# Linear-attention levels and diagonal in blocks of their own, and reordered stage starts, heads and merge operands, in a four-layer transformer kernel on one core

## The chip, the core and the metric

The kernel runs on one core of one Trainium2 chip. It is one program that computes a stack of four transformer layers. The metric is the device time of one execution in microseconds, lower is better; the median of several executions is compared. The engines are TensorE (PE, with its weight loads as PEld), VectorE (DVE), ScalarE (ACT), GpSimd (POOL) and SyncE (SP), which issues the transfers.

## What is computed

512 tokens of width 1024, float32 everywhere. The first block is a gated linear attention layer and a convolutional feed-forward layer, then a sparse attention layer (compressed keys, selected blocks, a window) and another convolutional feed-forward layer. The second block is two hybrid layers (four heads of differential attention and eight heads of stick-breaking attention side by side), each followed by a feed-forward layer. Each layer normalizes its input by its root mean square and adds its result to the residual x. The reference, cut to the mixers that the change touches:

```python
def gla_mixer(h, ...):                      # 4 heads, key width 128, value width 256
    q, k, v, r, a_low = split(h @ w_in)
    log_a = log_sigmoid(a_low @ w_alpha_up + b_alpha) / 16
    # b = cumulative sum of log_a over tokens, per head and key dimension
    # att[t, s] = sum_d q[t,d] * k[s,d] * exp(b[t,d] - b[s,d])   for s <= t
    ...
def hybrid_layer(x, ...):
    h = rms_norm(x, g_attn)
    dq, dk, dv, sq, sk, sv, gates = split(h @ w_in)
    # differential: softmax(q1 k1) v - lam * softmax(q2 k2) v, causal; then rms_norm
    # stick-breaking: z = q k / 8; a = exp(log_sigmoid(z) + sum over later keys of log_sigmoid(-z))
    merged = g_diff * (o_diff @ w_o_diff) + g_sb * (o_sb @ w_o_sb)
    x = x + merged @ w_out
    h2 = rms_norm(x, g_ffn)
    gate, up = split(h2 @ w_ffn_in)
    return x + (silu(gate) * up) @ w_ffn_out
```

## The kernel before, in words

**Layout.** Features lie on the 128 partitions and the 512 tokens in the free dimension, so x is eight tiles of 128 x 512. The stages run one after another: linear attention (gla), feed-forward, sparse attention (its keys and values, kv, then its queries and output), feed-forward, hybrid layer 0 (hyb0) and its merge, feed-forward, hybrid layer 1 (hyb1) and its merge, feed-forward.

**Weights.** All weight matrices are stored as 446 units of 128 x 1024, taken in a fixed order through a ring of four slots. SyncE issues the transfer of a unit into w_raw once the slot is free (s_used); POOL splits it into a high part w_hi and a remainder w_lo (L461, L464) and raises s_w. The activations are split likewise: XH and XL. A `tile` on TensorE is one unit: eight contraction blocks k, each of three matmuls of 128 x 512 into one bank (`product`, L488 to L490: high by XH, high by XL, low by XH).

**Start of a stage.** VectorE makes XL[k] block by block (L1657) and adds up the squares, ss (L1669), behind which `stats` (L504) sums ss over the partitions on TensorE. Its result gives rstd, by which every product of the stage is scaled when it is copied out of its bank. In kv, hyb0 and hyb1 the first tile waits for each XL[k] (s_xl), and `stats` stands behind tile 1.

**Linear attention.** The sum over s <= t inside a chunk of 128 tokens is split into seven levels: level lv pairs the odd and even halves of blocks of 128 >> lv tokens. For each level VectorE makes exponents (L1783, L1784), ScalarE takes the exponential, VectorE multiplies by queries and keys (`decayed`, L1789, L1790) into g_z, TensorE forms the products (L603) of every chunk (4) and head (4) at full width in banks 5 to 7, and VectorE places them into g_att through a mask (`place`, L1812). One level goes after each of the tiles 10 to 16; the same token with itself (`diagonal`, L613) comes after tile 17. Then TensorE turns the decayed keys (`end_keys`) and forms the outputs from g_att. In between VectorE copies the value tiles out (L1770) and TensorE turns them (L509).

**Hybrid layers.** TensorE runs 12 tiles, then 16 units of differential scores (n = 0 to 15), between which the groups of the further tiles are laid by `fill(t, part)`, 6 groups (one k each) a unit from tile 12 on. Then come eight stick-breaking heads. Head h is `s_scores`, two fill tiles 24+2h and 25+2h, a wait for `sp` (h_sp_lo, made by VectorE, L2249), the cumulative sums (L1090); ScalarE then takes the exponential. In heads 0 and 7 the tile 25+2h was cut: six groups ahead of the sums, two behind.

```python
cut = KT if 0 < h < SB_HEADS - 1 else 6
fill(25 + 2 * h, range(cut))
if h == 0:
    d_sumsq(DIFF_HEADS - 1)
pe.wait_ge(hs["sp"], k0 + h + 1)
```

A fill tile is copied out by VectorE (L2168, h_gate or h_raw), after a wait for its bank. The differential outputs h_od get their high part h_odh from ScalarE and the remainder h_odl from VectorE (L2258), four subtractions after the last head; the merge begins with them, then takes h_osl of the stick-breaking outputs. The engines run in program order, and semaphores order them among each other.

## Time and profile before

| what | value |
| --- | --- |
| median of 3 runs | 2874.49 us (2873.88 to 2876.15) |
| the profiled execution | 2872.57 us, of which the span of the trace is 2870.8 |
| TensorE | 2826.8 us busy, 98% of the span; weight loads 2278.6 |
| VectorE | 1346.0 us, 47% |
| ScalarE | 809.7 us, 28% |
| POOL | 2038.8 us, 71% |
| mean granted TensorE clock | 0.997 of full speed |
| transfers | 84 GB/s on average |

Busy time is an engine's own work in the span; the modelled end of a matmul lies somewhat after the moment at which the next one can start, so a timeline is better read from start to start. A row of the timeline has the start, the duration, the engine and line, the operands (out<-in) and in square brackets the idle time ahead of it with what ended it. A matmul of plain float32 operands is two records in the trace, so its counts there are twice those of the program (32 for a level's 16); one of split operands (XH, w_hi) is one.

### The profile page before, as it was taken

What the parts mean: (1) busy time and instruction counts of PE and PEld (TensorE: products, weight loads), DVE (VectorE), ACT (ScalarE), POOL (GpSimd) and SP (SyncE); (2) the same over time, 40 slices, a digit from 0 to 9 for tenths busy, and PEclk for the clock granted to TensorE, in tenths of its full rate; (3) what the DMA queues carried; (4) which work ended last, traced back from release to release, by engine and by line L of the source; (5) the groups of instructions that cost most, each with busy time, mean ns of one, the idle gap of its engine ahead of it and who ended that gap; (6) DMA issues with size and microseconds to landing.
All of it is one profiled execution on the core that took longest, in us unless ns stands there. A gap on an engine that the chain in (4) does not pass through costs nothing.

```text
span 2870.8 us, 38439 instructions
## 1 busy us (share of the span) xinstructions
PE 2826.8 (98%) x13860; PEld 2278.6 (79%) x13860; DVE 1346.0 (47%) x1980; ACT 809.7 (28%) x1477; POOL 2038.8 (71%) x2346
## 2 busy tenths in 40 slices
PE   9999999999999999999999999999999999999998
PEld 7888888878756888887777778888877777888887
DVE  3854666035576466613764453232065444623201
ACT  2242222023476222201434432110043444211101
POOL 6748989779635688877845577777786455877774
PEclk9999999999999999999999999999999999999999
DMA  4112222223200233222221222232222122222222
GB/s 156 61 49 92 99 97 95 95 91 116 81 2 2 74 97 100 96 95 95 82 67 59 67 88 96 95 99 99 95 92 78 59 67 73 90 99 97 95 95 95
DMA packets 66360, 242.54 MB, mean 84 GB/s; under 512 B 7488, under 2 KB 7616, under 8 KB 66240
## 3 DMA queue, kind: packets, MB, share of 16 engines
q1 hardware_dynamic: 66240, 240.95, 25.2%
q8 instruction: 74, 1.21, 0.2%
q14 instruction: 46, 0.38, 0.0%
HBM read 238.82 MB, written 2.10 MB: 84 GB/s over the span
## 4 chain that ended last, share of the span: by engine, by line
PE 90%; DVE 6%; POOL 2%; issue 1%; ACT 1%; DMA 0%; SPq 0%; DVEq 0%; ACTq 0%
PE bank L488 26%; PE bank L490 26%; PE bank L489 26%; POOL w_lo L464 1%; PE bank L912 1%; PE bank L837 1%; PE bank L1090 1%; PE bank L854 1%; DVE ss L1669 1%; PE bank L603 1%; PE bank L1005 1%; DVE XL L1657 1%; PE bank L1048 1%; PE bank L1061 1%; PE bank L986 1%
## 5 line engine op out<-in xcount | busy, mean ns | idle before, releaser
L464 POOL TENSOR_TENSOR w_lo<-w_raw,w_hi 128x256 fp32r<-128x256 f32 x1784 | 1482.5, 862 | 35.8
L461 POOL CAST w_hi<-w_raw 128x1024 fp32r<-128x1024 f32 x446 | 488.6, 1096 | 686.3 <-DMA w_raw<-weights_dram 685.6
L488 PE MATMUL bank<-XH,w_hi 128*128 128x512 f32 x2416 | 958.1, 397 | 9.0 <-DVE XL L1657 4.3
L490 PE MATMUL bank<-XH,w_lo 128*128 128x512 f32 x2416 | 942.4, 390 | 0.0
L489 PE MATMUL bank<-XL,w_hi 128*128 128x512 f32 x2416 | 941.9, 390 | 0.0
L488 PEld LDWEIGHTS bank<-XH,w_hi 128*128 128x128 f32 x2416 | 454.4, 188 | 113.6 <-issue 10.1
L490 PEld LDWEIGHTS bank<-XH,w_lo 128*128 128x128 f32 x2416 | 454.1, 188 | 96.4
L489 PEld LDWEIGHTS bank<-XL,w_hi 128*128 128x128 f32 x2416 | 454.7, 188 | 93.8 <-issue 2.6
L1680 DVE TENSOR_TENSOR X<-X,bank 128x512 f32<-128x512 f32 x64 | 43.8, 684 | 512.6 <-PE bank L490 512.3
L490 PE MATMUL bank<-hid_h,w_lo 128*128 (+1 forms) x704 | 273.9, 389 | 0.0
L488 PE MATMUL bank<-hid_h,w_hi 128*128 (+1 forms) x704 | 273.9, 389 | 0.0
L489 PE MATMUL bank<-hid_l,w_hi 128*128 (+1 forms) x704 | 273.9, 389 | 0.0
L1713 DVE TENSOR_TENSOR f_c<-bank,rstd 128x512 f32<-128x512 f32 x88 | 60.9, 692 | 293.3 <-PE bank L490 284.3
L1224 ACT ACTIVATE hid_h<-f_h 128x512 f32 x88 | 55.7, 632 | 397.0 <-DVE f_h L1728 397.0
L488 PEld LDWEIGHTS bank<-hid_h,w_hi 128*128 128x128 f32 x704 | 132.1, 188 | 27.6
L489 PEld LDWEIGHTS bank<-hid_l,w_hi 128*128 128x128 f32 x704 | 132.1, 188 | 27.5
L490 PEld LDWEIGHTS bank<-hid_h,w_lo 128*128 128x128 f32 x704 | 132.1, 188 | 27.2
L474 POOL TENSOR_SCALAR n_P<-n_P,n_st,n_gate 128x128 f32<-128x128 f32 (+3 forms) x112 | 69.8, 624 | 83.8 <-DVE n_st L2066 82.8
L1216 ACT ACTIVATE f_c<-f_u,par_sb 128x512 f32<-128x512 f32 x88 | 71.9, 817 | 169.2 <-DVE f_u L1713 169.1
L1222 ACT ACTIVATE f_s<-f_c 128x512 f32<-128x512 f32 x88 | 55.7, 633 | 192.4 <-DVE f_c L1713 147.4
L1730 DVE TENSOR_TENSOR hid_l<-f_h,hid_h 128x512 f32 x88 | 71.3, 810 | 81.0 <-ACT hid_h L1224 81.0
L1722 DVE SCALAR_TENSOR_TENSOR f_c<-f_u,par_sb,f_c 128x512 f32<-128x512 f32 x88 | 102.8, 1168 | 12.7 <-DVE f_c L1719 0.3
(348 smaller groups left out, 3374.7 us busy)
## 6 DMA issues: line engine op xcount, KB each, us to landing
w_raw<-weights_dram SPq DMA_DIRECT2D x446, 512.0 KB, 3.4
x_tok<-x_dram SPq DMA_DIRECT2D x4, 512.0 KB, 5.7
out_dram<-y_tok SPq DMA_DIRECT2D x4, 512.0 KB, 4.0
const_sb<-consts_dram SPq DMA_DIRECT2D x1, 834.0 KB, 11.6
par_sb<-params_dram SPq DMA_DIRECT2D x1, 665.0 KB, 10.0
masks_in<-masks_dram SPq DMA_DIRECT2D x1, 640.0 KB, 12.6
y_gain<-gain_out_dram SPq DMA_DIRECT2D x1, 512.0 KB, 6.1
const_sb<-consts_dram SPq DMA_DIRECT2D x1, 129.0 KB, 2.1
```

The costliest lines, as they stand in the source:

```text
L461: nc.gpsimd.tensor_copy(w_hi[s][:, :, :], w_raw[s][:, :, :]).then_inc(s_hi, 1)
L464: ins = nc.gpsimd.tensor_tensor(w_lo[s][:, rows, :], w_raw[s][:, rows, :], w_hi[s][:, rows, :].bitcast(F32), ALU.subtract)
L474: nc.gpsimd.tensor_scalar(w, w, n_st[:, 1, m:m + 1], n_gate[:, i, col:col + 1], ALU.mult, ALU.mult)\
L488: nc.tensor.matmul(out_ap, w_hi[slot][:, j, :], xh, start=start, stop=False)
L489: nc.tensor.matmul(out_ap, w_hi[slot][:, j, :], xl, start=False, stop=False)
L490: return nc.tensor.matmul(out_ap, w_lo[slot][:, j, :], xh, start=False, stop=stop)
L1216: nc.scalar.activation(f_c[side][:, :], f_u[side][:, 2:T + 2], ACT.Identity, bias=par_sb[:, bass.ds(t + b0, 1)], scale=par_sb[:, bass.ds(t ...
L1222: nc.scalar.activation(f_s[:, :], f_c[0][:, :], ACT.Silu).then_inc(s_silu, 1)
L1224: nc.scalar.activation(hid_h[:, bass.ds(i * (2 * T) + p * T, T)], f_h[:, :], ACT.Copy)\
L1713: V.tensor_tensor(dst, bank[2 * p + side][:, :], rstd[:, :], ALU.mult).then_inc(s_u, 1)
L1722: V.scalar_tensor_tensor(f, f_u[side][:, 0:T], par_sb[:, bass.ds(c + w0, 1)], f, ALU.mult, ALU.add).then_inc(s_c2, 1)
L1730: V.tensor_tensor(hid_l[:, bass.ds(i * (2 * T) + p * T, T)], f_h[:, :], hid_h[:, bass.ds(i * (2 * T) + p * T, T)].bitcast(F32), ALU.subtract)\
```

## The change

**Levels and diagonal.** The products of a level no longer fill 128 x 128 squares of which a mask keeps a part. Level 0 is one block of 64 x 64 for each chunk and head, level 1 two blocks of 32 x 32, and levels 2 to 6 and the diagonal four blocks of 32 keys (32 x 16 and 32 x 32). The four blocks of a chunk and head go to the four groups of 32 partitions of the bank. A level then fits one bank. `place` copies levels 0 and 1 straight to g_att, and puts levels 2 to 6 and the diagonal through one masked copy each into the compact g_ac, from which `spread` writes four copies to g_att. ScalarE's and VectorE's waits count accordingly.

**Starts.** In kv, hyb0 and hyb1 the first two tiles are interleaved block by block, the second two blocks behind (`first_tiles`), and `stats` stands inside tile 2, ahead of its third block.

**Heads.** Two groups of tile 12 go ahead of the first differential scores; tile 25+2h is no longer cut; and VectorE makes the four h_odl in the last head ahead of the copy of tile 38.

The diff, cut to its core (waits of later steps left out; of `place` the removed lines stand in the functions above):

```diff
+GB = 32
...
+        g_ac = at("g_ac", [P, TT, H4, GB], F32, o_A + 25088)
...
+            def first_tiles(u, k_sem, k_base):
+                lag = 2
+                pe.wait_ge(s_w, u + 1)
+                for k in range(KT + lag):
+                    if k < KT:
+                        pe.wait_ge(k_sem, k_base + k + 1)
+                        mm = product(bank[0][:, :], u % RING, k, XH[:, k, :], XL[:, k, :], k == 0, k == KT - 1)
+                    if k == KT - 1:
+                        mm.then_inc(s_used, 1)
+                    if k == lag:
+                        pe.wait_ge(s_w, u + 2)
+                    if k >= lag:
+                        j = k - lag
+                        mm = product(bank[1][:, :], (u + 1) % RING, j, XH[:, j, :], XL[:, j, :], j == 0, j == KT - 1)
+                mm.then_inc(s_used, 1)
+            def tile(u, b, xh, xl, k_sem=None, k_base=0, norm=None):
                 pe.wait_ge(s_w, u + 1)
                 for k in range(KT):
+                    if k == 2 and norm is not None:
+                        stats(norm)
...
                 def level(lv):
                     pe.wait_ge(gs["Z"], lv + 1)
-                    for pair in range(2):
-                        m = 2 * lv + pair
-                        if m >= 3:
-                            pe.wait_ge(gs["ev"], 2 * m - 4)
-                        for c in (2 * pair, 2 * pair + 1):
-                            for h in range(H4):
-                                z = g_z[lv % 2][:, h, c * P:(c + 1) * P]
-                                odd = z.rearrange("p (n two e) -> p n two e", two=2, e=P >> (lv + 1))[:, :, 1, :]
-                                to = c % 2 * 2 * P + h * P // 2
-                                mm = nc.tensor.matmul(bank[5 + m % 3][:, to:to + P // 2], z, odd, start=True, stop=True)
+                    m = lv + 1 if lv else 0
+                    if m >= 3:
+                        pe.wait_ge(gs["ev"], m - 2)
+                    for c in range(TT):
+                        for h in range(H4):
+                            z, n = g_z[lv % 2][:, h, c * P:(c + 1) * P], c * H4 + h
+                            if lv == 0:
+                                to = n % 8 * 64
+                                mm = nc.tensor.matmul(bank[5 + c // 2][0:64, to:to + 64], z[:, 0:64], z[:, 64:P],
+                                                      start=True, stop=True)
+                            elif lv == 1:
+                                for b in (0, 64):
+                                    mm = nc.tensor.matmul(bank[7][b:b + GB, n * GB:(n + 1) * GB], z[:, b:b + GB],
+                                                          z[:, b + GB:b + 2 * GB], start=True, stop=True)
+                            else:
+                                for b in range(0, P, GB):
+                                    odd = z[:, b:b + GB].rearrange("p (n two e) -> p n two e", two=2, e=P >> (lv + 1))[:, :, 1, :]
+                                    mm = nc.tensor.matmul(bank[5 + m % 3][b:b + GB, n * GB // 2:(n + 1) * GB // 2],
+                                                          z[:, b:b + GB], odd, start=True, stop=True)
+                        if lv == 0 and c % 2:
+                            mm.then_inc(gs["mm"], 1)
+                    if lv:
                         mm.then_inc(gs["mm"], 1)
...
                 def diagonal():
+                    pe.wait_ge(gs["ev"], LEVELS - 1)
                     for c in range(TT):
-                        m = 2 * LEVELS + c
-                        pe.wait_ge(gs["ev"], 2 * m - 4 if c < 3 else 4 * LEVELS + 1)
                         for h in range(H4):
-                            cols = slice(c * P, (c + 1) * P)
-                            mm = nc.tensor.matmul(bank[5 + m % 3][:, h * P:(h + 1) * P], g_k[:, h, cols], g_q[:, h, cols],
-                                                  start=True, stop=True)
-                        mm.then_inc(gs["mm"], 1)
+                            n = c * H4 + h
+                            for b in range(0, P, GB):
+                                cols = slice(c * P + b, c * P + b + GB)
+                                mm = nc.tensor.matmul(bank[7][b:b + GB, n * GB:(n + 1) * GB], g_k[:, h, cols], g_q[:, h, cols],
+                                                      start=True, stop=True)
+                    mm.then_inc(gs["mm"], 1)
...
                 for t in range(U_NSA_KV):
                     if t >= 4:
                         pe.wait_ge(ns["evac"], t - 3)
-                    tile(KV_UNIT[t], t % 4, XH, XL, s_xl if t == 0 else None, 8 * PREP[2])
-                    if t == 1:
-                        stats(2)
+                    if t == 0:
+                        first_tiles(KV_UNIT[0], s_xl, 8 * PREP[2])
+                    elif t > 1:
+                        tile(KV_UNIT[t], t % 4, XH, XL, norm=2 if t == 2 else None)
...
                 for t in range(12):
...
-                    tile(u0 + t, t % 5, XH, XL, s_xl if t == 0 else None, 8 * PREP[n0 if ly else MID])
-                    if t == 1:
-                        stats(n0 if ly else MID)
+                    if t == 0:
+                        first_tiles(u0, s_xl, 8 * PREP[n0 if ly else MID])
+                    elif t > 1:
...
+                fill(12, (0, 1))
...
-                    for p_ in range(6 * n, 6 * n + 6):
+                    for p_ in range(6 * n if n else 2, 6 * n + 6):
...
-                    cut = KT if 0 < h < SB_HEADS - 1 else 6
-                    fill(25 + 2 * h, range(cut))
+                    fill(25 + 2 * h)
...
-                    if cut < KT:
-                        fill(25 + 2 * h, range(cut, KT))
                     if h == 0:
                         s_scores(1)
...
                 def place(lv):
+                    if lv == 0:
+                        for m in range(2):
+                            dve.wait_ge(gs["mm"], m + 1)
+                            V.tensor_copy(g_att[0:64, 2 * m:2 * m + 2, :, 64:P].rearrange("p c h t -> p (c h) t"),
+                                          bank[5 + m][0:64, :].rearrange("p (q t) -> p q t", t=64)).then_inc(gs["ev"], 1)
+                        return
+                    m = lv + 1
+                    dve.wait_ge(gs["mm"], m + 1)
+                    products = bank[5 + m % 3]
+                    if lv == 1:
+                        for b in (0, 64):
+                            ins = V.tensor_copy(g_att[b:b + GB, :, :, b + GB:b + 2 * GB].rearrange("p c h t -> p (c h) t"),
+                                                products[b:b + GB, :].rearrange("p (q t) -> p q t", t=GB))
+                        ins.then_inc(gs["ev"], 1)
+                        return
+                    if lv > 2:
+                        dve.wait_ge(gs["ev"], lv + 1)
+                    to = g_ac[:, :, :, :].rearrange("p c h t -> p (c h) t")
                     if lv < LEVELS:
+                        e = P >> (lv + 1)
+                        to = to.rearrange("p q (n two e) -> p q n two e", two=2, e=e)[:, :, :, 1, :]
+                        products = products[:, 0:8 * GB].rearrange("p (q n e) -> p q n e", q=16, e=e)
+                        mask = masks_bf[:, lv:lv + 1, 0:GB // 2].bitcast(U16).broadcast_to([P, 16, GB // 2])\
+                            .rearrange("p q (n e) -> p q n e", e=e)
+                    else:
+                        products = products[:, :].rearrange("p (q t) -> p q t", q=16)
+                        mask = masks_bf[:, lv:lv + 1, 0:GB].bitcast(U16).broadcast_to([P, 16, GB])
+                    V.copy_predicated(to, mask, products).then_inc(gs["ev"], 1)
+                def spread():
+                    dve.wait_ge(gs["ev"], LEVELS + 2)
+                    for b in range(0, P, GB):
+                        ins = V.tensor_copy(g_att[b:b + GB, :, :, b:b + GB].rearrange("p c h t -> p (c h) t"),
+                                            g_ac[b:b + GB, :, :, :].rearrange("p c h t -> p (c h) t"))
+                    ins.then_inc(gs["ev"], 1)
...
                 V.memset(g_att[:, :, :, :], 0.0)
+                V.memset(g_ac[:, :, :, :], 0.0)
...
+                spread()
                 evac(18)
...
+                    for k in range(4 if h == SB_HEADS - 1 else 0):
+                        dve.wait_ge(hs["odh"], 4 * ly + k + 1)
+                        V.tensor_tensor(h_odl[:, k, :], h_od[:, k, :], h_odh[:, k, :].bitcast(F32), ALU.subtract)\
+                            .then_inc(hs["odl"], 1)
                     evac(24 + 2 * h)
```

What each engine issues shows three places.

TensorE in the linear attention, around level 2; a row is an instruction with its operands, then output partitions by streamed columns, and how many such follow each other. Before:

```order
L489 MATMUL bank<-XL,w_hi_60 128x512
L490 MATMUL bank<-XH,w_lo_56 128x512
L509 MATMUL bank<-const_sb,g_vt 128x128 x4
L603 MATMUL bank<-g_z_87 128x64 x16
L488 MATMUL bank<-XH,w_hi_61 128x512
```

After:

```order
L493 MATMUL bank<-XL,w_hi_60 128x512
L494 MATMUL bank<-XH,w_lo_56 128x512
L532 MATMUL bank<-const_sb,g_vt 128x128 x4
L634 MATMUL bank<-g_z_87 32x16 x64
L492 MATMUL bank<-XH,w_hi_61 128x512
```

The 16 matmuls of 128 x 64 became 64 of 32 x 16; the tiles around them stand as before (level 0 is now 16 of 64 x 64, level 1 is 32 of 32 x 32, the diagonal 64 of 32 x 32).

VectorE in the same loop, from the placing of one level to the exponents two levels later. Before:

```order
L1812 COPY_PREDICATED g_att<-masks_bf,bank 128x8x32 x4
L1783 TENSOR_TENSOR g_z_88<-g_b 128x128x8
L1784 TENSOR_TENSOR g_z_88<-g_b 128x128x8
L1770 TENSOR_TENSOR g_vt<-bank,rstd 128x512
L1789 TENSOR_TENSOR g_z_88<-g_z_88,g_q 128x128x8
L1790 TENSOR_TENSOR g_z_88<-g_z_88,g_k 128x128x8
L1812 COPY_PREDICATED g_att<-masks_bf,bank 128x16x16 x4
L1783 TENSOR_TENSOR g_z_87<-g_b 128x256x4
```

After:

```order
L1842 COPY g_att<-bank 32x16x32 x2
L1820 TENSOR_TENSOR g_z_88<-g_b 128x128x8
L1821 TENSOR_TENSOR g_z_88<-g_b 128x128x8
L1807 TENSOR_TENSOR g_vt<-bank,rstd 128x512
L1826 TENSOR_TENSOR g_z_88<-g_z_88,g_q 128x128x8
L1827 TENSOR_TENSOR g_z_88<-g_z_88,g_k 128x128x8
L1858 COPY_PREDICATED g_ac<-masks_bf,bank 128x16x16
L1820 TENSOR_TENSOR g_z_87<-g_b 128x256x4
```

Four masked copies a level became one with the same number of elements in each row (levels 0 and 1: two plain copies); everything else kept its place.

TensorE at the start of kv. Before, the end of tile 1, the statistics matmul (bank 7) and tile 2:

```order
L488 MATMUL bank1<-XH_50,w_hi0_60 128x512
L489 MATMUL bank1<-XL_51,w_hi0_60 128x512
L490 MATMUL bank1<-XH_50,w_lo0_56 128x512
L504 MATMUL bank7<-ss_67,const_sb_64 128x512
L488 MATMUL bank2<-XH_50,w_hi1_61 128x512
L489 MATMUL bank2<-XL_51,w_hi1_61 128x512
L490 MATMUL bank2<-XH_50,w_lo1_57 128x512
```

After, a piece of the interleaved tiles:

```order
L492 MATMUL bank1<-XH_50,w_hi0_60 128x512
L493 MATMUL bank1<-XL_51,w_hi0_60 128x512
L494 MATMUL bank1<-XH_50,w_lo0_56 128x512
L492 MATMUL bank0<-XH_50,w_hi3_63 128x512
L493 MATMUL bank0<-XL_51,w_hi3_63 128x512
L494 MATMUL bank0<-XH_50,w_lo3_59 128x512
```

And after, the statistics inside tile 2:

```order
L492 MATMUL bank2<-XH_50,w_hi1_61 128x512
L493 MATMUL bank2<-XL_51,w_hi1_61 128x512
L494 MATMUL bank2<-XH_50,w_lo1_57 128x512
L527 MATMUL bank7<-ss_67,const_sb_64 128x512
L492 MATMUL bank2<-XH_50,w_hi1_61 128x512
```

Bank 0 and bank 1 now take turns, and the statistics come two groups of three matmuls later in the order. The same stands at the start of hyb0 and hyb1.

VectorE in the last stick-breaking head. Before:

```order
L2232 TENSOR_TENSOR h_sp<-h_sp,const_sb 128x256
L2168 TENSOR_TENSOR h_gate<-bank,rstd 128x512
L2241 COPY h_a<-h_sp 128x128
L2242 COPY h_a<-h_sp 128x128
L2243 TENSOR_TENSOR h_a<-h_sp 128x128
L2244 TENSOR_TENSOR h_a<-h_sp,h_a 128x256
L2246 CAST h_later_hi<-h_a 128x640
L2247 TENSOR_TENSOR h_later_lo<-h_a,h_later_hi 128x640
L2249 TENSOR_TENSOR h_sp_lo<-h_sp,h_sp_hi_184 128x1280
L2168 TENSOR_TENSOR h_gate<-bank,rstd 128x512
L2258 TENSOR_TENSOR h_odl<-h_od,h_odh 128x512 x4
L2262 TENSOR_TENSOR h_osl<-h_os,h_osh 128x512 x3
```

After:

```order
L2288 TENSOR_TENSOR h_sp<-h_sp,const_sb 128x256
L2293 TENSOR_TENSOR h_odl<-h_od,h_odh 128x512 x4
L2224 TENSOR_TENSOR h_gate<-bank,rstd 128x512
L2301 COPY h_a<-h_sp 128x128
L2302 COPY h_a<-h_sp 128x128
L2303 TENSOR_TENSOR h_a<-h_sp 128x128
L2304 TENSOR_TENSOR h_a<-h_sp,h_a 128x256
L2306 CAST h_later_hi<-h_a 128x640
L2307 TENSOR_TENSOR h_later_lo<-h_a,h_later_hi 128x640
L2309 TENSOR_TENSOR h_sp_lo<-h_sp,h_sp_hi_185 128x1280
L2224 TENSOR_TENSOR h_gate<-bank,rstd 128x512
L2318 TENSOR_TENSOR h_osl<-h_os,h_osh 128x512 x3
```

The four h_odl moved up, ahead of both gate copies and of h_sp_lo.

## Rows read from the trace of the kernel before

**Rows 1.** The page, busy time by engine: busy us, share of the span, instructions.

```profile
PE 2826.8 (98%) x13860; PEld 2278.6 (79%) x13860; DVE 1346.0 (47%) x1980; ACT 809.7 (28%) x1477; POOL 2038.8 (71%) x2346
```

**Rows 2.** Waits of TensorE: engine, line, releaser: us in total, times, longest.

```profile
PE bank L488 <- DVE XL L1657: 4.3, 9, 0.9
...
PE bank L488 <- DVE h_odl L2258: 2.9, 2, 1.5
```

**Rows 3.** Grouping by line and form, TensorE: busy us, mean ns | idle us.

```profile
L603 PE MATMUL bank<-g_z 128*128 128x64 f32 x224 | 25.8, 273 | 0.0
...
L613 PE MATMUL bank<-g_q,g_k 128*128 128x128 f32 x32 | 3.7, 275 | 0.0
```

**Rows 4.** Timeline of TensorE, levels 0 and 1: start, duration, [idle before].

```profile
83.85 3.68 PE L603 MATMUL bank<-g_z 128*128 128x64 f32 x32
87.34 0.47 PE L488 MATMUL bank<-XH,w_hi 128*128 128x512 f32 x1
...
93.35 3.68 PE L603 MATMUL bank<-g_z 128*128 128x64 f32 x32
```

**Rows 5.** Timeline of VectorE in the linear attention.

```profile
73.89 1.76 DVE L1828 MEMSET g_att<- 128x2048 f32 x1 [2.56 <-ACT g_b L1251]
...
88.37 2.06 DVE L1789 TENSOR_TENSOR g_z<-g_z,g_q 128x1024 f32<-128x1024 f32 x1 [1.38 <-ACT g_z L1255]
...
101.44 1.43 DVE L1812 COPY_PREDICATED g_att<-masks_bf,bank 128x256 f32<-128x256 uint16 x4
...
135.08 1.82 DVE L1789 TENSOR_TENSOR g_z<-g_z,g_q 128x1024 f32<-128x1024 f32 x1 [1.38 <-ACT g_z L1255]
136.82 1.75 DVE L1790 TENSOR_TENSOR g_z<-g_z,g_k 128x1024 f32<-128x1024 f32 x1
...
159.60 0.69 DVE L1770 TENSOR_TENSOR g_r<-bank,rstd 128x512 f32<-128x512 f32 x1 [2.57 <-PE bank L490]
```

**Rows 6.** Timeline of TensorE, compressed values of the sparse stage.

```profile
732.27 1.11 PE L783 MATMUL bank<-par_sb,n_hid 128*32 128x64 f32 x64
733.31 0.66 PE L509 MATMUL bank<-const_sb,n_raw 128*128 128x128 f32 x4
```

**Rows 7.** Timeline of TensorE, start of the kv stage.

```profile
622.71 0.39 PE L488 MATMUL bank<-XH,w_hi 128*128 128x512 f32 x1
...
637.53 1.12 PE L504 MATMUL bank<-ss,const_sb 128*128 128x512 f32 x2 [0.73 <-DVE ss L1669]
638.09 0.80 PE L488 MATMUL bank<-XH,w_hi 128*128 128x512 f32 x1
```

**Rows 8.** Timeline of TensorE, heads of the second hybrid layer.

```profile
2174.60 0.49 PE L1005 MATMUL bank<-h_dk,h_dq 64*128 64x128 f32 x4 [0.94 <-DVE h_raw L2168]
...
2288.68 0.84 PE L1090 MATMUL bank<-h_sp_hi,negtri_r 128*128 128x512 f32 x3 [1.20 <-DVE h_sp_lo L2249]
...
2293.39 0.66 PE L1048 MATMUL bank<-h_sqs,h_sk 64*128 64x512 f32 x1 [0.83 <-issue]
...
2402.03 0.85 PE L1090 MATMUL bank<-h_sp_hi,negtri_r 128*128 128x512 f32 x3 [0.42 <-DVE h_sp_lo L2249]
...
2407.39 0.47 PE L488 MATMUL bank<-h_odh,w_hi 128*128 128x512 f32 x1 [1.47 <-DVE h_odl L2258]
```

**Rows 9.** Timeline of VectorE, heads of the second hybrid layer.

```profile
2288.90 0.75 DVE L2200 SCALAR_TENSOR_TENSOR h_od<-bank,h_sub,h_ors 128x512 f32<-128x512 f32 x1 [0.27 <-ACT h_ors L1613]
2292.59 0.69 DVE L2168 TENSOR_TENSOR h_gate<-bank,rstd 128x512 f32<-128x512 f32 x1 [2.94 <-PE bank L490]
...
2397.57 0.69 DVE L2168 TENSOR_TENSOR h_gate<-bank,rstd 128x512 f32<-128x512 f32 x1 [4.71 <-PE bank L490]
...
2406.57 2.49 DVE L2258 TENSOR_TENSOR h_odl<-h_od,h_odh 128x512 fp32r<-128x512 f32 x4
```

**Rows 10.** TensorE after its longest wait for weights: timeline; then one stretch with its granted clock.

```profile
709.15 0.47 PE L488 MATMUL bank<-XH,w_hi 128*128 128x512 f32 x1 [1.71 <-POOL w_lo L464]
...
709.90:713.30 3.40, 3.40 (x10) 0.51 0.12 45
```

More of the change, by code:

```diff
@@ L117, in constants @@
     lv = np.zeros((P, 8, P))
-    for n in range(LEVELS):
+    key, token = np.arange(P)[:, None] % GB, np.arange(GB)[None, :]
+    for n in range(2, LEVELS):
         h = P >> (n + 1)
-        lv[:, n] = (a // (2 * h) == b // (2 * h)) & ((a // h) % 2 == 0) & ((b // h) % 2 == 1)
-    lv[:, 7] = a == b
+        level = (key // (2 * h) == token // (2 * h)) & ((key // h) % 2 == 0) & ((token // h) % 2 == 1)
+        lv[:, n, 0:GB // 2] = level[:, (np.arange(GB) // h) % 2 == 1]
+    lv[:, 7, 0:GB] = key == token
     masks = np.concatenate([lv, np.where(b <= a, 0.0, NEG)[:, None], np.where(a < b, 0.0, NEG)[:, None]], axis=1)
@@ L2253, in hybrid @@
                     evac(25 + 2 * h)
-                for k in range(4):
-                    dve.wait_ge(hs["odh"], 4 * ly + k + 1)
-                    V.tensor_tensor(h_odl[:, k, :], h_od[:, k, :], h_odh[:, k, :].bitcast(F32), ALU.subtract)\
-                        .then_inc(hs["odl"], 1)
                 for a in range(3):
```

29 lines of the change are left out of this document (6 added, 23 removed).

## The prediction, made before the changed kernel was timed

> **What bounds the kernel now.** I read the page first: TensorE has work in 2826.8 of the 2870.8 us [rows 1], so only two things can shorten the program: fewer microseconds of TensorE work, or fewer of its 44 us of idling. The list of what TensorE waits for comes second. Two of its rows are touched by the change as a whole, XL at the start of a stage (4.3 us) and h_odl at the merge (2.9 us) [rows 2]; the others it touches (ss, h_raw, h_sp_lo) stand in brackets in the timelines [rows 7, 8]. A wait costs more than its row says, because a matmul's modelled end lies about 0.16 us behind the moment at which the next could have started; I therefore count from start to start in the timeline. A group of three 512-column matmuls (one k of a tile) takes 0.68 us, a tile 5.45 us. Third, in the linear attention, the grouping by form and the timelines of TensorE and VectorE show whether the work taken away there is on the path.
>
> **Linear attention, TensorE.** A level is 32 records and takes 87.34 - 83.85 = 3.49 us, 109 ns a record, and the next begins at 93.35, a cycle of 9.50 us [rows 3, 4]. The seven levels are 224 records, the diagonal 32 at the same pace (its 3.7 us of busy time end in the drain; I take 3.5) [rows 3]. After the change level 0 is 32 records with 64 weight columns, level 1 is 64 with 32 columns on two strips, levels 2 to 6 and the diagonal are 128 each on four strips. The nearest row is L783: 64 records with 32 weight columns on four strips, all in 733.31 - 732.27 = 1.04 us, 16.3 ns each [rows 6]. I take that: 128 x 16.3 ns = 2.1 us for a level (1.4 saved) and for the diagonal (1.4 saved). Level 1 uses half as many strips: 64 x 32.5 ns = 2.1 us (1.4 saved). Level 0 has half the columns in both operands: half of 109 ns, 1.75 us (1.7 saved). On TensorE alone this is 1.7 + 6 x 1.4 + 1.4 = 11.5 us. Bounds: below, the products here stream 16 or 32 columns, not the 64 of L783, so down to a third of 2.1 us, 0.7; above, four strips share the 109 ns of a full record, 27.3 ns each, 3.5 us a level, which is no gain at all.
>
> **Linear attention, VectorE.** TensorE cannot have all of it, since each level waits for operands that VectorE makes. VectorE never waits for TensorE between 88 and 139 us; it starts its cycle at 88.37 and for the fifth time after that at 135.08, 9.34 us a cycle, barely shorter than TensorE's 9.50 [rows 5]. So the new cycle is VectorE's. Of it the change takes away only the placing: four predicated copies in 1.43 us, 0.33 from one start to the next [rows 5], become one of the same size. That is 1.0 us less for levels 2, 3 and 4, whose placing lies ahead of the last level. Levels 0 and 1 are placed by two copies of 512 columns out of a bank, about 0.62 us each like the row of h_gate (0.69 with its end) [rows 9]: 0.1 less each. The clearing of g_ac adds about 0.4, a quarter of g_att's 1.76 us for a quarter of its elements [rows 5]. Together the operands of level 6 are ready 3.0 + 0.2 - 0.4 = 2.8 us earlier: they were ready at 136.82 + 1.75 = 138.57 [rows 5], now at 135.8. Level 6 began at 83.85 + 6 x 9.50 = 140.85, so it begins 5.0 us earlier; it is itself 1.4 shorter and so is the diagonal. The diagonal's mask is now one copy, and the four copies of spread (at most 4 x 0.69 = 2.8 us) fall into a stretch in which VectorE idled 2.57 us and had three mask copies more [rows 5]; TensorE needs them only after a tile of 5.45 us, so I cost them at nothing. Without that cover they would cost up to 2.8. Term: 5.0 + 1.4 + 1.4 = **7.8 us**, bounds 3.4 (only levels 0 and 1 gain) and 10.6 (levels at 0.7).
>
> **Starts of the three stages (kv, hyb0, hyb1).** The first tile began at 622.71; two tiles without a wait are 16 x 0.68 = 10.9 us, 633.6; but the statistics matmul ran at 637.53, after XL in the first tile and then ss, and the work went on at 638.09 [rows 7]. Interleaving units 0 and 1 gives each XL[k] 1.36 us instead of 0.68 and hides those waits. (Unit 1 is needed from the third step on, 4 to 5 us earlier than before; should POOL not have split it yet, up to 2.3 us of that would vanish in the next wait.) But the sum of squares, the end of VectorE's chain, doesn't come earlier: the statistics stay at 637.53. What the change does gain is that the two tiles and two groups of tile 2 are done by then: 2 x 0.68 = 1.36 us. The XL wait turns into a longer ss wait, 637.53 - 635.0 = about 2.3 us against 0.9. Three stages: **4.1 us**; the rotation and weight chains behind follow TensorE's release of its tiles. Bounds 0 (they don't follow) and 3 x 2.5 = 7.5 (a shorter ss chain).
>
> **Heads.** The score products of the first differential head waited 0.94 us for h_raw, some 1.1 from start to start [rows 8]; two groups of fill(12) go ahead of it, 1.36 us of work, so the wait is filled and the scores begin 0.3 later: 1.1 saved per layer, **2.2 us**. In stick-breaking head 0 two groups move ahead of the wait for h_sp_lo, which ends at 2288.68 [rows 8] whatever TensorE does; they were 1.36 us behind it, and then s_scores(1) waited until 2293.39 for the gate tile, copied out at 2292.59 + 0.69 [rows 8, 9]. With the tile done before the sums, its copy follows d_out, which ran at 2288.90 [rows 9]; d_out's sum of squares is now issued 1.3 us later, so d_out runs at 2290.2 to 2290.9 and the copy to 2291.5. s_scores(1) starts at 2291.6 and I take a little less than the difference: 1.7 per layer, **3.4 us**, bounds 1.3 and 2.4.
>
> **End of the heads.** The last head's sums ran at 2402.03 after a wait of 0.42, then two groups, and the merge began at 2407.39 after 1.47 of waiting for h_odl [rows 8]. Now the groups fill the first wait, so the sums begin at 2402.8 and end 2.25 us later, and h_odl (2.49 us in four) is computed where VectorE idled 4.71 us for the gate tile [rows 9]. The merge can begin at 2405.05: 2.3 per layer, **4.7 us**. If the four subtractions ran later than that gap they would push h_sp_lo of head 7 by as much; the cover is 4.7 against 2.5.
>
> **The clock.** TensorE waited 1.71 us at 709.15, and for the next 3.4 us the granted clock was 0.51, the lower of its two levels, 1.2 GHz, which lost 1.7 us [rows 10]. The new ss waits of kv and hyb0 (2.3 us each) are longer than that one; the waits of 1.5 us and less in these rows were not followed by a fall. I count one such loss, **-1.7 us**. The Trainium skill, TensorE: Matmul & The Clock Gate, Part 1, says idling brings the lower clock and renewed activity releases it; the trace agrees, 0.51 after the wait.
>
> **The sum.** 7.8 + 4.1 + 2.2 + 3.4 + 4.7 - 1.7 = 20.5 us. The profiled execution took 2872.57 us in all (2870.8 span), 1.9 below the median of 2874.49. So 2872.57 - 20.5 = 2852.1, and as a median **2854.0 us**.
>
> **Rivals.**
> - *Small products are no cheaper than a quarter of a full one* (27.3 ns, above): the linear attention gives 3.4 instead of 7.8, 2858.4 us. For it: no row has so few streaming columns, and loading weights may set the pace. Against: L783's 16.3 ns. Chance 17%. The Trainium skill, TensorE: Matmul & The Clock Gate, section Back-to-back issue gap, has a floor of about 25 ns for 1 to 64 columns: by it a level takes 3.2 us, and the whole sum would be about 18 us. L783's 16.3 ns already lie under that floor, so the trace disagrees where strips are shared.
> - *The level loop is as fast as TensorE alone*, or no clock falls: 10.6 in the first term and no loss, 2849.5 us. Against: VectorE's 9.34 us cycle. 12%.
> - *More falls of the clock*: the loop gets seven waits of 1 to 2 us beside sparse small products; three or four more losses of 1.7 us, part of them hidden since TensorE waits there anyway: 2859 us. 10%.
> - *Slower*: the small products cost so much that the level loop outweighs the rest. The other parts save 12.7 after the clock; 6 blocks of 128 records lose that at (3.5 + 2.4) / 128 = 46 ns a record. One mechanism: each strip's weight load waits for the matmul before it instead of overlapping, so a record costs about 59 ns; a block is then 7.6 us, 4.1 over 3.5, and the program 2874.5 + 24.6 - 14.4 = 2885 us. Only L783 against it, but plainly. 2%.
> - *Nothing measurable* (several gains given back later, within 5.7 us): 3%.
> - The forecast itself, 2850 to 2858: 56%.
>
> **Numbers.** 0.2% of this kernel is 5.7 us, about what a measurement of it can tell from no change. Leaving 20% outside, I take 2849 to 2861. Faster 0.95, same 0.03, slower 0.02.
>
> **What would show it.** After: level records at some 16 ns and TensorE waiting for g_z in each level, 1 to 2 us; the diagonal's end 7.8 us earlier; the statistics matmul of kv still some 15 us behind the first tile, with one wait of about 2.3 us and none for XL; no wait for h_odl; s_scores(1) 2.9 us behind the first sum of head 0, not 4.7. I am wrong if the levels' records stand at 27 ns or more, if VectorE's cycle stays at 9.3 us, or if the clock is below 1.00 in the level loop.

## The result, and the profile after

| | median | runs | ratio to before, 95% interval |
| --- | --- | --- | --- |
| before | 2874.18 us | 4 (2869.63 to 2876.15) | |
| changed | 2856.53 us | 4 (2851.03 to 2858.23) | 0.9943 [0.993, 0.9955] |

The change made the kernel 17.7 us faster (13 to 20 by the interval); the forecast was 2854.0, in a range of 2849 to 2861. The profiled execution took 2858.23 us with a span of 2856.4, 14.4 less than that of before. The sum is right; the paths to it are only in part those of the forecast.

The page, busy time by engine, against [rows 1]:

```profile
PE 2811.7 (98%) x14468; PEld 2265.6 (79%) x14468; DVE 1338.3 (47%) x1963; ACT 809.8 (28%) x1477; POOL 2044.0 (72%) x2346
```

TensorE has 15 us less work, and about as much idling as before (44.7 us, before 44.0). What it waits for, against [rows 2] (engine, line, releaser: us, times, longest):

```profile
PE bank L1129 <- DVE h_sp_lo L2309: 4.1, 2, 2.1
PE bank L527 <- DVE ss L1706: 3.8, 2, 1.9
PE bank L492 <- POOL w_lo L468: 3.5, 5, 1.7
PE bank L634 <- DVE g_z L1827: 3.4, 3, 1.7
```

The waits for XL and h_odl are gone. In their place stand waits for ss (3.8, before 2.2), for h_sp_lo (from 3.3 in four to 4.1 in two) and for g_z, and more for the split weights (1.7 before).

**Linear attention.** Timeline of TensorE, levels 0, 2 and 3, the diagonal and the first outputs, against [rows 4]:

```profile
85.69 2.08 PE L625 MATMUL bank<-g_z 128*64 128x64 f32 x32 [0.19 <-DVE g_z L1827]
...
102.56 1.27 PE L634 MATMUL bank<-g_z 128*32 128x16 f32 x128 [1.16 <-DVE g_z L1827]
...
112.48 1.91 PE L634 MATMUL bank<-g_z 128*32 128x16 f32 x128 [1.75 <-DVE g_z L1827]
...
144.17 1.30 PE L649 MATMUL bank<-g_q,g_k 128*32 128x32 f32 x128
...
152.37 0.79 PE L684 MATMUL bank<-g_att,g_v 128*128 128x128 f32 x5
```

128 records of a level take 1.27 us, 9.9 ns each (level 3 ran at the lower clock); TensorE waits 1.16 and 1.75 us for g_z ahead of levels 2 and 3, 0.19, 0.20 and 0.53 ahead of levels 0, 1 and 6, and not at all ahead of 4 and 5. From the first level to the first outputs it was 76.86 us (83.85 to 160.71) and is now 66.68. Timeline of VectorE in this loop, against [rows 5]: an operation on g_z, the placing, another operation on g_z, this one beside POOL's work, and the spreading:

```profile
95.13 1.21 DVE L1820 TENSOR_TENSOR g_z<-g_b 128x1024 f32<-128x1024 f32 x1
...
112.35 0.43 DVE L1858 COPY_PREDICATED g_ac<-masks_bf,bank 128x256 f32<-128x256 uint16 x1
...
113.82 2.05 DVE L1821 TENSOR_TENSOR g_z<-g_b 128x1024 f32<-128x1024 f32 x1
...
148.34 3.88 DVE L1864 COPY g_att<-g_ac 32x512 f32<-32x512 f32 x4
```

The placing fell from 1.43 to 0.43 us as forecast, and VectorE's cycle from 9.34 to 8.53 us (`decayed` starts at 90.95 and for the fifth time after that at 133.60). An operation of `exponents` on 1024 columns is 1.21 or 2.05 us long. The spreading took 3.88, not the 2.8 that I allowed, and ended at 152.22, 0.15 us ahead of the outputs at 152.37; that it cost nothing was a near thing.

**Start of kv**, timeline of TensorE, against [rows 7]:

```profile
614.43 0.39 PE L492 MATMUL bank<-XH,w_hi 128*128 128x512 f32 x1
...
616.87 0.50 PE L492 MATMUL bank<-XH,w_hi 128*128 128x512 f32 x1 [0.24 <-POOL w_lo L468]
...
629.23 1.13 PE L527 MATMUL bank<-ss,const_sb 128*128 128x512 f32 x2 [1.85 <-DVE ss L1706]
...
700.28 0.77 PE L492 MATMUL bank<-XH,w_hi 128*128 128x512 f32 x1 [1.70 <-POOL w_lo L468]
```

From first tile to statistics it is 14.80 us (before 14.82), with waits of 0.24 and 1.85 in place of five, much as forecast. Two groups of tile 2 are done by then. The 0.24 is a wait for unit 1, which POOL had not split yet (0.73 in hyb0 and 0.30 in hyb1), as the forecast had allowed. But the last row shows that the wait for split weights later in the stage, 1.71 in [rows 10], is still there.

**End of the heads**, second hybrid layer. Timeline of VectorE, against [rows 9]:

```profile
2380.78 4.30 DVE L2293 TENSOR_TENSOR h_odl<-h_od,h_odh 128x512 fp32r<-128x512 f32 x4 [2.22 <-ACT h_odh L1612]
2385.01 0.68 DVE L2224 TENSOR_TENSOR h_gate<-bank,rstd 128x512 f32<-128x512 f32 x1
...
2387.18 1.54 DVE L2307 TENSOR_TENSOR h_later_lo<-h_a,h_later_hi 128x640 fp32r<-128x640 f32 x1
2388.64 2.01 DVE L2309 TENSOR_TENSOR h_sp_lo<-h_sp,h_sp_hi 128x1280 fp32r<-128x1280 f32 x1
```

Timeline of POOL beside it:

```profile
2380.35 4.19 POOL L468 TENSOR_TENSOR w_lo<-w_raw,w_hi 128x256 fp32r<-128x256 f32 x4
```

Timeline of TensorE, against [rows 8]:

```profile
2390.70 0.85 PE L1129 MATMUL bank<-h_sp_hi,negtri_r 128*128 128x512 f32 x3 [2.03 <-DVE h_sp_lo L2309]
...
2392.94 0.48 PE L492 MATMUL bank<-h_odh,w_hi 128*128 128x512 f32 x1
```

The four subtractions took 4.30 us and not 2.49; the gate copy behind them came 1.75 us late (2397.57 in [rows 9], less the 14.31 by which the kernel was ahead there, is 2383.26), h_later_lo took 1.54 and h_sp_lo 2.01 where they take 0.83 and 1.48 in the version with h_odl behind them (below). TensorE waited 2.03 for h_sp_lo, and the wait at the merge had only moved.

**By stretches.** The changed kernel was measured a second time, on another chip (2856.28 us, against 2872.73 for the kernel before; ratio 0.9946 [0.9933, 0.996]), and gave a second trace. I expected its stretches to repeat to 0.1 us outside the first 70 us, the falls of the clock and the starts, and a start to be 13 or 15 us in any kernel; the rival was that each kernel has a fixed value. The rival is refuted (hyb0's start took 13.36 us once and 15.04 the other time), but starts of 14.26 and 14.33 show that there are more than two values, and "heads" of layer a differed by 0.4.

The next table takes starts from the timelines of nine of the profiled executions, so that a late beginning in one of them doesn't count (us; "levels" is first level to g_osq, "start" first tile to statistics, "heads" from the matmul of h_lam to s_scores(1), "end" from there to the first merge matmul, a and b the two hybrid layers). Executions of like code differ mostly in "start" and where the clock fell.

| kernel | levels | start kv / a / b | heads a / b | end a / b |
| --- | --- | --- | --- | --- |
| before | 110.96 | 14.82 / 14.88 / 12.93 | 147.94 / 148.25 | 114.02 / 114.00 |
| changed | 100.87 | 14.80 / 13.36 / 14.93 | 145.79 / 145.22 | 113.92 / 113.85 |
| changed, second trace | 100.89 | 14.26 / 15.04 / 14.83 | 145.40 / 145.21 | 115.16 / 113.86 |
| levels alone | 101.33 | 12.87 / 12.93 / 14.95 | 148.32 / 147.56 | 114.01 / 114.02 |
| order alone | 110.94 | 14.00 / 14.24 / 14.92 | 145.24 / 145.33 | 114.96 / 113.77 |
| starts undone | 100.92 | 14.83 / 14.93 / 14.87 | 145.40 / 145.63 | 113.86 / 113.83 |
| h_odl last | 100.92 | 14.88 / 14.96 / 14.94 | 145.74 / 145.62 | 111.61 / 111.56 |
| h_odl behind h_sp_lo | 100.90 | 14.91 / 14.33 / 13.99 | 145.71 / 145.70 | 111.60 / 111.57 |
| copies for splits | 100.90 | 12.24 / 12.24 / 12.24 | 145.36 / 145.42 | 113.89 / 114.81 |

### The profile page after: what moved, and what is told of

Same layout as the page of the kernel before. It is cut to its first block, busy times and chain, and to the rows that moved or that the text cites. A ratio compares the mean times of both kernels' runs of the same rounds, so it can differ in the third digit from the quotient of the medians.

```text
span 2856.4 us, 39615 instructions
## 1 busy us (share of the span) xinstructions
PE 2811.7 (98%) x14468; PEld 2265.6 (79%) x14468; DVE 1338.3 (47%) x1963; ACT 809.8 (28%) x1477; POOL 2044.0 (72%) x2346
## 3 DMA queue, kind: packets, MB, share of 16 engines
q8 instruction: 79, 1.29, 0.2%
## 4 chain that ended last, share of the span: by engine, by line
PE 88%; DVE 6%; POOL 2%; ACT 2%; issue 1%; DMA 0%; SPq 0%; DVEq 0%; ACTq 0%
PE bank L492 26%; PE bank L494 25%; PE bank L493 25%; POOL w_lo L468 2%; PE bank L950 1%; PE bank L875 1%; PE bank L1129 1%; PE bank L892 1%; PE bank L1045 1%; PE bank L1088 1%; PE bank L1101 1%; DVE XL L1694 1%; PE bank L1026 1%; DVE ss L1706 1%; POOL w_hi L465 1%
## 5 line engine op out<-in xcount | busy, mean ns | idle before, releaser
L1759 DVE SCALAR_TENSOR_TENSOR f_c<-f_u,par_sb,f_c 128x512 f32<-128x512 f32 x88 | 105.6, 1200 | 12.8 <-DVE f_c L1756 0.3
## 6 DMA issues: line engine op xcount, KB each, us to landing
masks_in<-masks_dram SPq DMA_DIRECT2D x1, 640.0 KB, 12.8
```

The lines of the kernel that those rows point to most:

```text
L1759: V.scalar_tensor_tensor(f, f_u[side][:, 0:T], par_sb[:, bass.ds(c + w0, 1)], f, ALU.mult, ALU.add).then_inc(s_c2, 1)
```

## The experiments

**The two halves apart.** The first keeps of the diff only the hunks of the linear attention (masks, g_ac, `level`, `diagonal`, `place`, `spread` and their waits), the second only the others.

> The kernel before with the linear-attention part of the change alone. Theory: the parts add up, and this one is worth what the trace of the changed kernel shows between the first level and the last output, 10.1 us; about 2864. Rival, the forecast's term with VectorE's cycle as the bound throughout: 7.8 us, about 2866.4. If levels and reordering help each other only together, less than 7.

> The kernel before with the reordered starts, heads and merge operands alone. Theory: the trace of the changed kernel gives -0.9 in the kv stage, 4.7 in hybrid layer 0 and 2.5 in hybrid layer 1, together 6.4 us; about 2867.8. Rival, the forecast's terms 4.1 + 2.2 + 3.4 + 4.7 - 1.7 = 12.7 us: 2861.5.

Levels alone: 2860.89 us, ratio 0.9966 [0.9954, 0.9978], which is 9.8 us (6 to 13) and holds the theory's 10.1 as well as the rival's 7.8; only the traces part the two. Order alone: 2867.25, ratio 0.9986 [0.9977, 0.9995], which is 4.0 us (1.4 to 6.6); that leaves out the forecast's 12.7 us and just holds my 6.4 (0.9978). The table gives the levels 9.6 to 10.1 us in every kernel that has them, so they don't need the other half.

**The starts undone.** `first_tiles` and the statistics inside tile 2 taken back (the edit in kv; hyb0 and hyb1 likewise):

```diff
-                    if t == 0:
-                        first_tiles(KV_UNIT[0], s_xl, 8 * PREP[2])
-                    elif t > 1:
-                        tile(KV_UNIT[t], t % 4, XH, XL, norm=2 if t == 2 else None)
+                    tile(KV_UNIT[t], t % 4, XH, XL, s_xl if t == 0 else None, 8 * PREP[2])
+                    if t == 1:
+                        stats(2)
```

> The changed kernel with the first two tiles of kv, hyb0 and hyb1 one after the other again and the statistics behind tile 1. Theory: the interleaving is worth little, since it only reaches the statistics sooner (1.36 us a stage) and kv gives that back in waits for split weights; slower by 0 to 2 us, 2857.5. Rival, the forecast's term: slower by 4.1 us, 2860.6.

2857.74 us, ratio 0.9952 [0.9938, 0.9966]; 1.2 us over the changed kernel, or 2.6 by the two ratios (0.9943 there), less than these runs can tell. The traces are finer: from the statistics to the next common point (mid_ss in layer a, h_lam in b) the interleaving is worth 1.36 us (11.87 against 10.51, 28.20 against 26.83, but for the second trace of the changed kernel, where the clock fell ahead of mid_ss). In kv, from the statistics to the compressed values, five kernels with it take 94.2 to 95.3 us and three without 93.1 to 94.7: its 1.36 us is given back, as far as single executions show. In the changed kernel a wait of 0.57 us for w_lo at 664.84 has come ahead of the one of 1.70 that remained.

**h_odl moved.** Once back behind the last head, once directly behind h_sp_lo and ahead of the copy of tile 39 (the same lines, removed from where the change put them):

```diff
+                    for k in range(4 if h == SB_HEADS - 1 else 0):
+                        dve.wait_ge(hs["odh"], 4 * ly + k + 1)
+                        V.tensor_tensor(h_odl[:, k, :], ..., ALU.subtract).then_inc(hs["odl"], 1)
                     evac(25 + 2 * h)
```

> The changed kernel with the four subtractions for h_odl back behind the last head. Theory: they stand ahead of h_sp_lo of head 7, take 1.07 us each while POOL splits weights, and TensorE's last sums wait 2 us for h_sp_lo; put behind, the sums run at once (2.2 us earlier in each layer), and the subtractions are done beside the sums. 2856.5 - 4.4 = about 2852. Rival: the merge waits for h_odl again (1.5 us a layer as before), 2855 or more, no gain that can be told.

> The changed kernel with the four h_odl directly behind h_sp_lo of head 7, ahead of the copy of tile 39. Theory: the sums run 2.2 to 2.4 us earlier in each layer, and the 0.8 us that the merge lost in the run with the subtractions behind the copy is gone; 4.8 us less than the changed kernel, about 2851.7. Rival: beside the split of a weight unit a subtraction takes 1.07 to 1.2 us against 0.68 us of TensorE's work on it, so the merge still waits 0.8 a layer: 2853.3.

Last: 2854.09 us, ratio 0.994 [0.9926, 0.9953], which by time can't be told from the changed kernel (0.9943). Behind h_sp_lo: 2850.35, ratio 0.9926 [0.9912, 0.9939], against 2856.28 for the changed kernel on the same chip, 0.9946 [0.9933, 0.996]; the intervals still overlap, and the traces carry the reading. In both the end of the heads is 2.3 us shorter per layer. With h_odl last, the merge then ran 0.8 us slower (46.98 us to its first matmul of h_mh against 46.18), at the pace of subtractions of up to 1.23 us beside POOL (median 1.22, shortest 0.68); behind h_sp_lo that went too (46.20). Timeline of VectorE in the second one:

```profile
2379.03 1.48 DVE L2305 TENSOR_TENSOR h_sp_lo<-h_sp,h_sp_hi 128x1280 fp32r<-128x1280 f32 x1
2380.43 4.96 DVE L2311 TENSOR_TENSOR h_odl<-h_od,h_odh 128x512 fp32r<-128x512 f32 x4
```

Timeline of TensorE:

```profile
2381.35 0.74 PE L1129 MATMUL bank<-h_sp_hi,negtri_r 128*128 128x512 f32 x3
...
2383.49 0.48 PE L492 MATMUL bank<-h_odh,w_hi 128*128 128x512 f32 x1
```

No wait is left at the sums, nor at the merge, though the subtractions take even longer (4.96).

**Whose work stretches VectorE's.** For four units at each of the three starts POOL copies instead of subtracting, so that the products with w_lo of these units are of other numbers (`few` is true for them):

```diff
+                    if few:
+                        ins = nc.gpsimd.tensor_copy(w_lo[s][:, rows, :], w_raw[s][:, rows, :])
```

> The changed kernel in which POOL, for four units at the start of each of kv, hyb0 and hyb1, copies the unit in place of subtracting (this changes the products with w_lo of these units). Theory: VectorE's XL and ss are slowed by POOL's two-operand subtractions; with copies a start takes 13 us or less in all three stages, XL is 0.74 us each and TensorE's wait for ss is below 0.3. Rival: the chain's length has to do with VectorE or ScalarE alone; starts stay between 13 and 15 us, with the ss wait of 1.9 in some.

All three starts take 12.24 us (one execution, 2846.38 us). That is TensorE's own work, 18 groups of 0.68 us without a wait: VectorE's chain is no longer what a start waits for. Timeline of VectorE at the start of hyb1, in the changed kernel:

```profile
2093.18 0.67 DVE L1717 TENSOR_TENSOR X<-X,bank 128x512 f32<-128x512 f32 x1
2093.78 1.32 DVE L1694 SCALAR_TENSOR_TENSOR XL<-X,par_sb,XH 128x512 fp32r<-128x512 f32 x1
```

And in this one, first while POOL stands idle, then beside its copies:

```profile
2081.89 0.68 DVE L1721 TENSOR_TENSOR X<-X,bank 128x512 f32<-128x512 f32 x1
2082.48 0.74 DVE L1698 SCALAR_TENSOR_TENSOR XL<-X,par_sb,XH 128x512 fp32r<-128x512 f32 x1
...
2085.00 1.78 DVE L1698 SCALAR_TENSOR_TENSOR XL<-X,par_sb,XH 128x512 fp32r<-128x512 f32 x2
```

Timeline of POOL beside it:

```profile
2084.39 1.04 POOL L465 CAST w_hi<-w_raw 128x1024 fp32r<-128x1024 f32 x1 [2.17 <-DMA w_raw<-weights_dram]
2085.50 3.15 POOL L470 CAST w_lo<-w_raw 128x256 fp32r<-128x256 f32 x4
```

XL, which reads two operands from the SBUF, takes 1.32 us where it meets POOL's subtractions, 0.89 beside its copies and 0.74 beside nothing; X, whose second operand comes from a bank, is 0.67 beside the subtractions and 0.68 beside nothing. So my "0.74 each" held only where POOL stood idle, but POOL's subtractions stretch VectorE more than its copies do. No wait for ss is left.

**The statistics later.** On top of h_odl behind h_sp_lo, `k == 2` in `tile` became `k == 6`:

> The same with the statistics of kv, hyb0 and hyb1 ahead of the seventh instead of the third block of tile 2. Theory: four groups of TensorE (2.7 us) fill the wait of 1.9 us for ss; the kv stage gives it back in waits for split weights, so 1.9 to 3.8 us less than without, 2848 to 2850. Rival: rstd comes later, the first tiles are copied out later and the wait returns at tile 5; no gain, 2851.7.

2846.32 us, ratio 0.9913 [0.99, 0.9927], the fastest version: 10 us below the changed kernel and 4 below the one without this edit, whose interval overlaps. TensorE of its kv stage:

```profile
627.64 1.02 PE L527 MATMUL bank<-ss,const_sb 128*128 128x512 f32 x2
...
643.93 0.30 PE L792 MATMUL bank<-n_yh,w_hi 128*128 128x130 f32 x1 [2.98 <-ACT n_yh L1370]
```

The wait for ss is gone; a new one of 2.98 us for n_yh stands 16 us behind it, so in kv the rival was right too, yet the stage as a whole, to the next stage's statistics, was 367.10 us against 369.34. That is no more than like executions differ by (369.16 and 370.39 for the changed kernel, 368.02 with h_odl last), and in the hybrid layers the first tile to h_lam took 42.20 and 40.69 us against 42.35 and 40.74. Where the 4 us come from is not shown.

**Who sets the pace of the levels.** VectorE's multiplication by the keys left out in levels 1 to 5 (their products are then of other numbers), and each product formed twice, or half of them twice (the signal behind level 0 is counted to match):

```diff
-                    for c in range(TT):
+                    for c in [c for c in range(TT) for _ in range(2)]:   # (0, 0, 1, 1, 2, 3) for half
```

> The changed kernel in which VectorE leaves out the multiplication by the keys in levels 1 to 5 (the products of these levels are then of other numbers). Theory: VectorE's round is 1.2 to 1.8 us shorter five times, and TensorE's waits for g_z (5.1 us) go: 4 to 5 us less between the first level and the last output, after which TensorE sets the pace. Rival, TensorE sets it already: less than 1 us.

> The changed kernel with the products of every level formed twice (in the same place, the result is the same). Read from the first level to the last output, 100.9 us in the changed kernel. Theory: VectorE sets the pace of the levels, TensorE waits 5.1 us for g_z in them; the second products cost 2.0 + 1.2 + 5 x 1.27 = 9.5 us, of which these waits take up 4 to 5, so 4.5 to 5.5 us longer. Rival, TensorE sets the pace: 9.5 us longer.

> The changed kernel with half of the products of every level formed twice: 192 records in a row in levels 2 to 6 in place of 128 (and of 256 in the run before, where TensorE stood still for 2.9 to 3.6 us within each of these levels, released by nothing that the trace shows). Read from the first level to the last output, 100.9 us in the changed kernel. Theory: what stopped TensorE there is the supply of its instructions, which falls behind only in a long row of very short ones; with 192 the stops are under 1 us each or gone, the 4.8 us of added products are mostly taken up by the waits for g_z, and the stretch is 101 to 105 us. Rival: the cost goes with the number of products (24.4 us for twice as many): 113 us.

Keys left out: "levels" takes 95.66 us, 5.2 less, and the waits are gone (TensorE, levels 2 to 4):

```profile
101.36 1.27 PE L634 MATMUL bank<-g_z 128*32 128x16 f32 x128
...
108.68 1.27 PE L634 MATMUL bank<-g_z 128*32 128x16 f32 x128
...
116.02 1.27 PE L634 MATMUL bank<-g_z 128*32 128x16 f32 x128
```

Levels now follow each other every 7.3 us, TensorE's own pace, against VectorE's 8.53. So VectorE sets the pace of the changed kernel's levels, by 5 us. (In time 2851.68 us, 0.9931 [0.9914, 0.9948].) Twice: "levels" takes 125.27 us, 24.4 more, and 2883.62 in all, 1.0047 [1.0031, 1.0063] (one of its five executions took 3488.97, for a reason that isn't known); neither of my two numbers. TensorE:

```profile
102.43 2.25 PE L635 MATMUL bank<-g_z 128*32 128x16 f32 x246
107.61 0.30 PE L635 MATMUL bank<-g_z 128*32 128x16 f32 x10 [2.93 <-issue]
...
113.94 2.00 PE L635 MATMUL bank<-g_z 128*32 128x16 f32 x216
119.03 0.53 PE L635 MATMUL bank<-g_z 128*32 128x16 f32 x40 [3.08 <-issue]
```

Within each of four levels it stood still for 2.9 to 3.6 us, released by nothing that the profile shows, each time some 30 records earlier than in the level before (after 246, 216, 187, 157), and once more for 2.45 us in the tile behind level 6. Half more: "levels" takes 110.69 us (2864.75 in all, 0.9981 [0.9971, 0.999]), outside my 101 to 105 and nearer to the rival's 113. Three levels ran their 192 records in 1.80 us without a stop inside, two stopped for 3.3 and 3.5 us, and a stop of 1.42 us came in a tile. So my "under 1 us each" was wrong; but records alone don't set the cost either, since equal levels of one trace stopped or didn't.

Counted through levels and tiles, the stops lie 254, 255, 254 and 383 records of TensorE apart with the products twice, and 254 and 636 with half of them: about 2, 3 and 5 times 127. The profile's queue of instructions carries 79 packets with 1.29 MB in the changed kernel, 82 with 1.34 in the second of these runs and 85 with 1.39 in the first, 16 KB each. A supply of instructions that comes in portions of fixed size fits both counts, but that it is what stops TensorE is argued: no run changed the supply alone.

## Why the prediction was right, and where it was not

- **Levels, 7.8 forecast, 10.1 measured** (keeping to 83.85 to 194.81 and 85.69 to 186.56). The mechanism was right: VectorE's pace, shown by the keys left out. Sizes were off: I took 16.3 ns a record and it is 9.9, so level 6 and the diagonal each gave 2.2 us, not 1.4; and level 6 came 5.85 earlier, not 5.0, as VectorE's operands for it were ready 3.6 us earlier and not 2.8. The 9.9 ns also rule out both rivals in which a record costs 27 ns or more. `spread`, which I cost at nothing, took 3.88 us and was covered by 0.15. Two of the waits for g_z lie in the 1 to 2 us that I expected in each level, the others at 0 to 0.53.
- **Starts, 4.1 forecast, 2.7 found.** 1.36 us per stage was exact in both hybrid layers. The step that failed is "the rotation and weight chains behind follow TensorE's release of its tiles": in kv they don't. There TensorE waits for units that POOL has yet to split, as in the longest wait for weights before [rows 10]; this is read from the waits (0.57 and 1.70 us), no run changed POOL's pace in this stretch.
- **Scores and head 0, 2.2 + 3.4 = 5.6 forecast, 5.2 found** ("heads", 147.9 and 148.3 to 145.8 and 145.2). Right: the waits for h_raw and for head 0's h_sp_lo are gone, and s_scores(1) comes 3.02 and 3.44 us behind the first sum of head 0, for 4.71 before and 2.9 forecast; a wait of 0.61 and 0.73 us is left there.
- **End of the heads, 4.7 forecast, 0.25 found** (114.0 to 113.9). The step that failed: "h_odl (2.49 us in four) is computed where VectorE idled 4.71 us". I took its duration from a place where POOL stood still; in the gap POOL was splitting a unit, and the gap only opens 2.2 us after the softplus work, when h_odh is there. Moving the lines back gave 2.3 us a layer, the forecast's own number.
- **The clock, -1.7 forecast.** The price was right where the fall came, and the forecast could not say where that would be. The waits of kv and hyb1 for ss (1.85 and 1.90 us) were followed by no fall in the changed kernel's first trace. In its second trace hyb0's wait for ss (2.15 us) was: the clock behind it was 0.50, and mid_ss came 12.14 us behind the statistics in place of 10.51, 1.6 us lost. In the first trace a fall came inside the level loop behind a wait of 1.75. That is one of the forecast's own signs of being wrong, "if the clock is below 1.00 in the level loop"; but it cost nothing there, since the next two levels then waited 0 instead of 1.0 and 0.5 us as in the run with h_odl last, which had no fall there. The new waits for h_sp_lo, which the forecast did not have, can bring a fall as well ("end" of 115.16 in place of 113.9).
- **The sum.** 10.1 + 2.7 + 5.2 + 0.25 = 18.3, against 17.7 measured: 2.3 too little in the levels stood against 4.4 too much at the end and 1.4 at the starts. That the forecast came out within 3 us is in part luck: a sum right by offset is no proof of its terms. Nor do the stretches hold everything. The reordered half is 8.2 of these 18.3 us, but alone it gave 4.0 (1.4 to 6.6). Left out are the way to the statistics (12.87 to 14.95 us in the table's traces without `first_tiles`, 13.36 to 15.04 in those with it, the run with POOL's copies apart) and the falls of the clock; how much each takes is not shown.

## What to carry to other kernels

Before work is moved into another engine's idle gap, look at what the neighbour engine does in that gap, and take the duration from a place where it does the same. Where a term is moved ahead of something that others wait for, price the whole queue behind it; four lines moved below h_sp_lo were worth more than the starts. And compare stretches from start to start in the traces: single parts of 1 to 2 us stood out there, which medians with a spread of 7 us could not show.

## What the runs showed of the hardware

- **VectorE and POOL slow each other.** XL takes 0.74 us alone and up to 1.32 beside POOL's subtractions, h_odl 0.62 and up to 1.53, a g_z operation 1.21 and up to 2.05, and a group of four of these subtractions takes POOL 2.8 us alone and up to 4.5 beside VectorE in the rows above. Not every operation that meets a subtraction is slowed. X, with one operand in a bank, keeps its time. The Trainium skill, GPSIMD Engine Reference, section 1. Specifications, says that the SBUF interfaces are shared with VectorE, with contention for VectorE's instructions of two SBUF inputs; the traces agree, 1.32 against 0.74 for those and 0.67 against 0.68 for one operand from a bank. That a start takes 12.9 us in one execution and 14.9 in another may come from the way in which the two engines meet; it isn't shown, and POOL works through 12.8 of the 12.9 us as well.
- **A wait of 2 us is not always followed by a slower clock.** The two profiled executions of the changed kernel have the same waits of 2.00 to 2.08 us for h_sp_lo, one a layer. Windows of 3 us (the granted clock is the third number from the end) in the first trace, behind the wait of 1.75 in the level loop and behind those two:

```profile
112.50:115.50 3.00, 3.00 (x131) 2.77 (x132) 3.00 (x3) 0.00 (x0) 2.20 (x2) 0.50 0.08 29
1639.70:1642.70 3.00, 3.00 (x20) 2.65 (x20) 0.00 (x0) 1.37 (x4) 2.92 (x5) 1.00 0.08 31
2391.50:2394.50 3.00, 3.00 (x21) 2.65 (x20) 0.00 (x0) 1.33 (x3) 2.92 (x5) 1.00 0.07 26
```

  In the second trace, behind hyb0's wait for ss and then behind the same two:

```profile
1352.50:1355.50 3.00, 3.00 (x7) 1.98 (x6) 2.69 (x4) 1.72 (x4) 2.92 (x4) 0.50 0.02 5
1639.20:1642.20 3.00, 3.00 (x15) 2.81 (x14) 0.00 (x0) 0.05 (x1) 2.92 (x5) 0.50 0.09 36
2392.20:2395.20 3.00, 3.00 (x21) 2.65 (x20) 0.00 (x0) 1.31 (x3) 2.92 (x5) 1.00 0.07 29
```

  Behind layer a's wait the clock was 1.00 in the one and 0.50 in the other; behind layer b's, 1.00. The Trainium skill, TensorE: Matmul & The Clock Gate, Part 1, says that the number of slow matmuls at a kernel's start varies from run to run of one kernel; these rows show the like behind a wait in the middle. Four runs of the changed kernel at mean clocks of 0.995 to 0.997 spread over 7.2 us.
- **Small products on four strips cost 9.9 ns a record** (32 weight columns, 16 streamed), below the 16.3 of [rows 6] and 19.8 ns for a matmul of the program, which is two records. The Trainium skill, TensorE: Matmul & The Clock Gate, section Back-to-back issue gap, gives a floor of about 25 ns from start to start. Neither count keeps to it here, so for products on four strips the measurement decides. Level 1, 32 columns each on two strips, took 1.21 us for 64 records, 19 ns.
- **192 or 256 of them in a row can stop TensorE for 3 us**; with 128 in a row there was at most one gap, 0.26 to 0.96 us behind 125 records of level 5, in the traces of four kernels.
